# A transformer kernel on one core: the table load moved ahead of the third weight split at each feed-forward's end, the fourth split moved behind the next layer's input

## The reference, cut to what matters

```python
def _rms(x, g):
    return x * lax.rsqrt(jnp.mean(x * x, axis=-1, keepdims=True) + EPS) * g

def _swiglu(xn, w_gate, w_up, w_down):
    return (jax.nn.silu(xn @ w_gate) * (xn @ w_up)) @ w_down

for i in range(4):                       # layers 0 and 3 conv, 1 pool, 2 attention
    g = norm_g[i]
    m = mixer_i(_rms(x, g[0]))
    x = x + _rms(m, g[1])
    f = _swiglu(_rms(x, g[2]), ffn_w_gate[i], ffn_w_up[i], ffn_w_down[i])
    x = x + _rms(f, g[3])
```

## Time and profile before

| | us |
|---|---|
| median of 3 runs | 2462.35 |
| lowest and highest of them | 2461.59, 2470.54 |
| the profiled execution's own time | 2461.79 |
| its span | 2460.0 |
| PE busy | 2325.7 (95%) |
| DVE busy | 1046.8 (43%) |
| ACT busy | 691.6 (28%) |

### The profile page before, as it was taken

One profiled execution on the slowest core, in us unless ns is written; L12 is line 12 of the kernel. 1 busy time (PEld: TensorE's weight loads), 2 busy tenths in 40 slices (PEclk: granted clock), 3 DMA queues, 4 the chain that ended last, 5 costly groups with the idle time before them and its releaser, 6 DMA issues.

```text
span 2460.0 us, 34059 instructions
## 1 busy us (share of the span) xinstructions
PE 2325.7 (95%) x13529; PEld 1575.6 (64%) x13529; DVE 1046.8 (43%) x1497; ACT 691.6 (28%) x945; POOL 4.9 (0%) x6
## 2 busy tenths in 40 slices
PE   7999899999999999999997999979999999999999
PEld 5677633333333333333334999969998899999998
DVE  7774231111111111111114766565555565576654
ACT  2121310110000110000104354454444544354443
POOL 0000000000000000000000000000000000000000
PEclk9999999999999999999998999989999999999999
DMA  8456379999999999999996455535554255554552
GB/s 361 153 206 239 148 310 422 422 422 422 422 422 422 422 422 422 422 422 422 422 422 271 177 197 188 185 114 201 188 188 171 102 177 185 187 180 172 180 183 99
DMA packets 97344, 682.20 MB, mean 277 GB/s; under 512 B 10692, under 2 KB 13528, under 8 KB 15224
## 3 DMA queue, kind: packets, MB, share of 16 engines
q1 hardware_dynamic: 94560, 673.36, 69.4%
q10 hardware_dynamic: 2712, 7.82, 0.9%
HBM read 680.00 MB, written 1.13 MB: 277 GB/s over the span
## 4 chain that ended last, share of the span: by engine, by line
PE 64%; DMA 30%; DVE 3%; ACT 2%; issue 1%; SPq 1%; ACTq 0%; DVEq 0%
DMA ring<-in_w_exp 28%; PE psum L530 13%; PE psum L531 13%; PE psum L532 13%; PE psum L847 8%; PE psum L598 3%; PE psum L699 2%; PE psum L871 2%; PE psum L737 1%; DVE arena L1688 1%; DMA ring<-in_w_ada 1%; PE psum L568 1%; DVE h L1682 1%; PE psum L824 1%; ACT ring_parts L1451 1%
## 5 line engine op out<-in xcount | busy, mean ns | idle before, releaser
L530 PE MATMUL psum<-x_parts,ring_parts 128*128 128x256 f32 x1920 | 546.0, 284 | 3.6 <-DVE arena_parts L1688 3.6
L531 PE MATMUL psum<-arena_parts,ring_parts 128*128 128x256 f32 x1920 | 544.8, 284 | 0.0
L532 PE MATMUL psum<-x_parts,ring_parts 128*128 128x256 f32 x1920 | 544.8, 284 | 0.0
L429 DVE TENSOR_TENSOR ring_parts<-ring,ring_parts 128x2048 fp32r<-128x2048 f32 x181 | 414.2, 2291 | 304.4 <-ACT ring_parts L1451 299.5
L847 PE MATMUL psum<-ring,arena 128*64 128x512 f32 x2176 | 487.9, 596 | 50.1 <-DMA ring<-in_w_exp 50.1
L847 PEld LDWEIGHTS psum<-ring,arena 128*64 128x64 f32 x2176 | 159.2, 136 | 337.5 <-issue 337.5
L530 PEld LDWEIGHTS psum<-x_parts,ring_parts 128*128 128x128 f32 x1920 | 370.1, 193 | 6.8 <-issue 5.4
L531 PEld LDWEIGHTS psum<-arena_parts,ring_parts 128*128 128x128 f32 x1920 | 370.2, 193 | 1.4
L532 PEld LDWEIGHTS psum<-x_parts,ring_parts 128*128 128x128 f32 x1920 | 369.9, 193 | 0.0
L1451 ACT ACTIVATE ring_parts<-ring 128x2048 fp32r<-128x2048 f32 x181 | 342.5, 1905 | 85.0 <-DMA ring<-in_w_mix 53.3
L1685 DVE TENSOR_SCALAR arena<-psum 128x512 f32<-128x512 f32 x68 | 47.0, 692 | 660.8 <-ACT arena L1429 453.5
(11 more groups left out here) (272 smaller groups left out, 1938.0 us busy)
## 6 DMA issues: line engine op xcount, KB each, us to landing
ring<-in_w_exp SPq DMA_DIRECT2D x408, 1024.0 KB, 23.0
ring<-in_w_ffn SPq DMA_DIRECT2D x132, 1024.0 KB, 4.8
ring<-in_w_mix SPq DMA_DIRECT2D x49, 1024.0 KB, 4.8
ring<-in_w_ada SPq DMA_DIRECT2D x24, 1024.0 KB, 6.4
ring<-in_w_in SPq DMA_DIRECT2D x16, 1024.0 KB, 9.5
arena<-gain_scratch ACTq DMA_DIRECT2D x10, 512.0 KB, 3.7
ring<-in_w_out SPq DMA_DIRECT2D x4, 1024.0 KB, 4.9
ring<-in_w_attn SPq DMA_DIRECT2D x2, 1024.0 KB, 4.8
```

The costliest lines, as they stand in the source:

```text
L429: return engine.tensor_tensor(ring_parts[:, s, :], ring[:, s, :], ring_parts[:, RAW + s, :], ALU.subtract)
L530: mm(out, w[0], a[0], start=start, stop=False, **more)
L531: mm(out, w[0], a[1], start=False, stop=False, **more)
L532: return mm(out, w[1], a[0], start=False, stop=stop, **more)
```

## The change

At the end of each feed-forward ACT's table load now stands ahead of `late_first(m + 2)`, and the split of piece m + 3 (the next layer's piece n + 3) is left out of the tail. It is put into the next layer instead: in layers 2 and 3 right behind `next_input`, in layer 1 behind the pooled input, each time just ahead of the split of piece n + 4. In layer 0 nothing is added, since the first four pieces are split before it. Layer 3's tail has no next pieces, and its `late_first` and `late_second` issue nothing. The number of instructions stays the same. PE and SyncE have the same queues as before.

```diff
--- before.py
+++ after.py
@@ -1522,6 +1522,8 @@
                 n = LAYER_AT[layer]
                 if layer in (0, 3):
                     next_input(g2[:, 4 * layer, :], 4, 5)
+                    if layer:
+                        late_first(n + AHEAD - 1)
                     for j in range(4):
                         for i in range(3):
                             late_first(n + 3 * j + i + AHEAD)
@@ -1541,10 +1543,11 @@
                         act.wait_ge(sem("pool_input"), c + 1)
                         go(pooled[0][:, c, :], psum[:, c % 4, 0:T], ACT.Copy, scale=g2[:, 4 * layer, c:c + 1]
                            ).then_inc(sem("cacc_high"), 1)
+                    late_first(n + AHEAD - 1)
                     late_first(n + AHEAD)
                 else:
                     next_input(g2[:, 4 * layer, :], 4, 5)
-                    for i in range(8):
+                    for i in range(-1, 8):
                         late_first(n + i + AHEAD)
                     act.wait_ge(sem("x_rstd"), at["x_norm"])
                     for i in range(8, 12):
@@ -1647,9 +1650,8 @@
                 gate_silu(it + FC2)
                 late_first(m + 1)
                 hidden_first(it + FC2, 0)
+                act.preload_act_table_set("natural_log_exp_and_others")
                 late_first(m + 2)
-                late_first(m + 3)
-                act.preload_act_table_set("natural_log_exp_and_others")
                 result_norm(0)
 
             for i, (t, half) in enumerate(REGIONS):
@@ -2158,9 +2160,11 @@
                         dve.wait_ge(sem("cacc_high"), KC + c + 1)
                         stt(pooled[1][:, c, :], psum[:, c % 4, 0:T], g2[:, 4 * layer, c:c + 1], pooled[0][:, c, :],
                             ALU.mult, ALU.subtract).then_inc(sem("cacc_low"), 1)
+                    late_second(n + AHEAD - 1)
                     late_second(n + AHEAD)
                 elif layer == 2:
                     next_input(g2[:, 4 * layer, :], 4)
+                    late_second(n + AHEAD - 1)
                     factor()
                     for i in range(8):
                         late_second(n + i + AHEAD)
@@ -2306,7 +2312,6 @@
                 up_pair(p - FFN_TAIL + 2, it + FC2, 0)
                 hidden_second(it + FC2, 0)
                 late_second(p + 2)
-                late_second(p + 3)
             add_result(0)
```

## The result

| | before | after |
|---|---|---|
| median, us | 2463.76 (22 runs) | 2468.64 (22 runs) |
| lowest and highest, us | 2457.87, 2470.9 | 2465.23, 2473.62 |
| the profiled execution, us | 2461.79 | 2469.35 |
| its span, us | 2460.0 | 2467.5 |

The ratio is 1.002 [1.0013, 1.0026]: the change costs 4.9 us (3.2 to 6.4), and 0.2% is no measurable change by the bound of 0.5%. I had forecast 2465.5 us, 3.15 above the median shown then. With 22 runs the kernel before stands at 2463.76 itself, so the difference was forecast 1.7 us too small.

The account below looks back on a forecast made before the run. PE was taken as the bound, other engines counting only where it waits for them. Terms -2.7 + 2.2 + 3.9 = +3.4 us on 2461.79 gave 2465.2, stated as 2465.5 us; range 2459 to 2471.

Parts of the forecast that it names:

- The ends, -2.7: Feed-forward ends of layers 0, 1 and 2: first residual add earlier, gaining 0.95, 0.95 and 0.8 us.
- The pool, +2.2: Layer 1, behind the pooled input: the added split delays the first result region, costing 2.2 us.
- Layers 2 and 3, +1.9 and +2.0: Starts of layers 2 and 3: the added split delays DVE's first PSUM read; PE waits 1.9 and 2.0 us.
- The clock: PE's granted clock: no fall expected in the new waits of 1.9 us, so no term in the sum.
- The rival with falls in the new waits: Layers 2 and 3: clock stays low for some pieces, 4.8 us each, over 0.5% slower from two; chance 0.03.
- Covered splits: Layers 1 to 3: slack hides the moved splits, only the 2.7 us gain is left, 2459.7 us; chance 0.12.
- The doubled load: Feed-forward ends: load holds ACT twice as long, gain falls to 0.7 us in all, 2467.7 us; chance 0.05.
- Layer 1's clock otherwise: Layer 1: clock stays full ahead of the pooling input, 2463.8 us, or low longer behind the mixer, 2467; chance 0.18.

Follow-up runs that it names:

- the split alone: Kernel after with the table load back behind the third split, the fourth split still out of the tail: 2467.37 us, ratio 1.0019 to the kernel before.
- the splits later: Kernel after, layer 1's splits of pieces n+3 and n+4 moved into the feed-forward input's wait for the spread factor: 2465.72 us, ratio 1.0011 to before.
- reads-first run: Kernel after, in layers 2 and 3 DVE's first PSUM read put ahead of the splits of pieces n+3 and n+4: 2461.98 us, ratio 0.9996 to before.
- the load alone: Kernel before with the table load ahead of the third split, the fourth split staying in the tail: 2467.04 us, ratio 1.0018 to before.
- the version that keeps the gain: Kernel after: layer 1's two splits and layers 2 and 3's copy of n+3 in spread-factor waits, first PSUM read ahead of n+4's split: 2458.07 us, ratio 0.997.

## Why the prediction was nearly right

**The ends, -2.7.** Right, with the wrong reason for a part of it. Measured from the hidden copy to PE's first matmul of the next layer's mixer, the end of layer 1 is 0.84 shorter (14.50 before, 13.66 after) and that of layer 2 0.70 (14.36, 13.66); the residual add at the end of layer 0 is 0.95 closer. Together -2.5. But the load contributes nothing to it, which the run with the split alone showed; my working put the load's end and the copy's in one step and never asked what the one would do without the other.

**The pool, +2.2.** Right: 2.19 in the timeline, 6.1 to 8.3 in PE's wait. The run with the splits later took both out (8.3 to 3.8).

**Layers 2 and 3, +1.9 and +2.0.** Right: from the mixer's first matmul to the third piece 1.81 and 1.97 us more. The reads-first run took both out.

These sum to -2.5 + 2.2 + 3.8 = +3.5, against the +3.4 forecast. What was timed is 4.9.

**The clock.** This is the step that failed: the sum has no term for it, by the sentence "So I expect no fall in the new waits of 1.9 us". The missing term is about 1.5 us, and the stages of the table say where. Layer 2's stage grew by 2.67 (means 146.02 and 148.69); its end and its wait account for -0.84 + 1.81 = 0.97, and the 1.70 left is one fall of 3.4 us, in all four profiles. Layer 3's grew by only 1.35 (121.16 and 122.51): its parts give -0.70 + 1.97 = 1.27, and the fall behind the new wait (1.6 us once the landing times told of at the end are taken off) is nearly set off in the mean by the earlier fall of before, 2.5 us in two of its three profiles. So the sentence was wrong about the new wait in layer 3, but what is missing in the sum is the fall behind layer 2's mixer, for which the prediction had no row. The pool's stage grew by 1.06. Together 5.1, where 4.9 (3.2 to 6.4) was timed.

I had taken one row with PE busy 1.31 of 2 us at full clock for the rule of all waits of that size, though PE's wait there was 1.33 us and not 1.9; in the profile of the load alone the clock fell behind that same wait (1850). The rival with falls in the new waits was right in kind and wrong in size: it needed two whole pieces, 9.6 us, to reach 0.5%, and the falls last 3.4 us and cost 1.7.

What isn't settled is why the clock falls behind layer 2's mixer in the kernel after. PE's two waits there are the same as before: in the kernel before

```profile
1973.34 1.32 PE L950 MATMUL psum<-con,arena 128*128 128x128 f32 x8 [1.42 <-DVE arena L1688]
...
1975.23 0.36 PE L530 MATMUL psum<-x_parts,ring_parts 128*128 128x256 f32 x1 [0.57 <-DVE arena_parts L1688]
```

and in the kernel after

```profile
1975.72 1.32 PE L950 MATMUL psum<-con,arena 128*128 128x128 f32 x8 [1.42 <-DVE arena L1690]
...
1977.61 0.35 PE L530 MATMUL psum<-x_parts,ring_parts 128*128 128x256 f32 x1 [0.57 <-DVE arena_parts L1690]
```

The load alone, which has no new wait in layer 2, fell there too (1976), and so did the version that keeps the gain (1970); the pool's splits later, which has one, did not. So the fall there doesn't need the new wait, though it is more frequent with it: five of six profiles, and two of eight without. That this is a cause isn't shown. A shift in time against something that these profiles don't show would fit; no run tested it.

**The rivals.** Covered splits fell with the two new rows of PE's waits. The doubled load fell with the 0.02 us behind it. Layer 1's clock otherwise fell as well: its stretches are 6.8 and 13.6 us in both kernels. The measured 2468.64 lies inside the range by bounds that were set for other terms; short falls of the clock weren't among them, so this much is luck.

## What to carry to other kernels

Moving work onto engines with slack costs nothing only where nothing that PE waits for is queued behind it: look for the first read or result behind the new place, and price the move by its slack, here 0.4 of 2.29 us. The place that was free here was the wait for a small result of another engine (the spread factor), where ACT and DVE both stand idle. When two edits come together, work out each without the other: the load's move was worth nothing with the split gone, and cost time with it in place.

## What the runs showed of the hardware

**Short falls of the clock.** Behind waits of 1.3 to 1.8 us the granted clock may or may not drop for 3.4 us at 1.2 GHz. Behind layer 2's mixer it came at nearly the same place in four of four profiles of the kernel after, and in none of three of the kernel before, whose waits there are as long. Each costs 1.7 us where PE is busy; the 6.8 us of before at 2162 to 2174, part of it in a wait, cost 2.5.

**A weight piece's landing varies, and passes to PE.** At the end of layer 3's mixer ACT's last copy waits for the landing of a feed-forward piece, and the statistics that PE waits for are queued behind that copy. In the kernel after, ACT's copy and PE's matmul in the profile shown:

```profile
2262.96 1.92 ACT L1451 ACTIVATE ring_parts<-ring 128x2048 fp32r<-128x2048 f32 x1 [1.94 <-DMA ring<-in_w_ffn]
...
2268.65 1.32 PE L950 MATMUL psum<-con,arena 128*128 128x128 f32 x8 [1.49 <-DVE arena L1690]
```

and in its fourth profile:

```profile
2263.80 1.92 ACT L1451 ACTIVATE ring_parts<-ring 128x2048 fp32r<-128x2048 f32 x1 [1.26 <-DMA ring<-in_w_ffn]
...
2269.49 1.32 PE L950 MATMUL psum<-con,arena 128*128 128x128 f32 x8 [0.69 <-DVE arena L1690]
```

ACT's wait was 1.94, 2.42, 1.75 and 1.26 us in the four profiles, PE's 1.49, 2.00, 1.29 and 0.69: the one follows the other 0.4 to 0.6 lower. In the kernel before it was 1.26, 2.15 and 2.34, with 0.70, 1.73 and 1.94 on PE, so this is a spread of 1.3 us between executions; no difference between the kernels is seen. With it the excess of layer 3's stage in before's second profile, 122.26 - 118.76 = 3.5, splits into 1.0 of landing and 2.5 of clock.
